# A hybrid SSD and attention layer: four gate tiles ahead of the merge, and the projection, its norms and the first feed-forward tiles in column halves

## What is computed

```python
hn = rmsnorm(x, p['norm_mix_pre']) * (1 + sc1) + sh1
proj = hn @ p['w_in']
z, xbc, dt, q, k, v, gates = jnp.split(proj, IN_SPLITS, axis=-1)
y_ssm, conv_new, h_new = ssm_branch(z, xbc, dt, conv_ctx, h0, p)
...
y_att = swa_prompt(q, k, v, sinks)
...
g_ssm, g_att = jnp.split(jax.nn.sigmoid(gates), 2, axis=-1)
merged = g_ssm * (y_ssm @ p['w_ssm_out']) + g_att * (y_att @ p['w_att_out'])
x = x + g1 * rmsnorm(merged @ p['w_out'], p['norm_mix_post'])
hn = rmsnorm(x, p['norm_ffn_pre']) * (1 + sc2) + sh2
gate, up = jnp.split(hn @ p['w_ffn_in'], 2, axis=-1)
gate, ffn_new = causal_dwconv(gate, ffn_ctx, p['ffn_conv_w'], p['ffn_conv_b'])
f = (jax.nn.silu(gate) * up) @ p['w_ffn_out']
x = x + g2 * rmsnorm(f, p['norm_ffn_post'])
```

## Time and profile before

| | |
|---|---|
| median of 3 runs (us) | 1429.63 (1429.2 to 1437.0) |
| profiled execution (us) | 1436.78 |
| its span, first to last instruction (us) | 1435.0 |
| mean granted clock of TensorE (share of full speed) | 0.959 |
| TensorE busy | 1339.5 us, 93% |
| VectorE busy | 809.9 us, 56% |
| ScalarE busy | 508.1 us, 35% |
| POOL busy | 530.9 us, 37% |
| DMA | 164.31 MB, mean 115 GB/s |

### The profile page before, as it was taken

One profiled execution on the slowest core, in us unless ns is written; L12 is line 12 of the kernel. 1 busy time (PEld: TensorE's weight loads), 2 busy tenths in 40 slices (PEclk: granted clock), 3 DMA queues, 4 the chain that ended last, 5 costly groups with the idle time before them and its releaser, 6 DMA issues. The chain is left out here.

```text
span 1435.0 us, 24802 instructions
## 1 busy us (share of the span) xinstructions
PE 1339.5 (93%) x10265; PEld 1255.5 (87%) x10265; DVE 809.9 (56%) x1288; ACT 508.1 (35%) x879; POOL 530.9 (37%) x315
## 2 busy tenths in 40 slices
PE   4699998999999999998798999988999999999996
PEld 1489988899899999998788999974899999999996
DVE  1745316898898898894780000337466666660105
ACT  2212425455455455453441222332332233332221
POOL 0533322332332333332464443332344444443443
PEclk8699989999999999999899999998799999999998
DMA  8275414433433433334331222541222222222221
GB/s 364 99 265 134 122 53 140 126 95 117 138 102 117 129 112 116 117 100 170 101 106 59 88 89 89 205 187 40 75 89 89 88 84 83 87 90 88 82 81 63
DMA packets 74015, 164.31 MB, mean 115 GB/s; under 512 B 28240, under 2 KB 42352, under 8 KB 70432
## 3 DMA queue, kind: packets, MB, share of 16 engines
q1 hardware_dynamic: 73904, 162.74, 35.2%
HBM read 147.10 MB, written 16.07 MB: 114 GB/s over the span
## 5 line engine op out<-in xcount | busy, mean ns | idle before, releaser
L161 POOL TENSOR_TENSOR w_lo<-raw_w,w_hi 128x1024 fp32r<-128x1024 f32 x174 | 429.0, 2466 | 730.3 <-ACT w_hi L155 730.3
L183 PE MATMUL psum<-hp_hi,w_hi 128*128 128x274 f32 x1472 | 449.8, 306 | 22.4 <-POOL hp_lo L284 13.4
L183 PE MATMUL psum<-hp_lo,w_hi 128*128 128x274 f32 x1472 | 430.9, 293 | 0.0
L183 PE MATMUL psum<-hp_hi,w_lo 128*128 128x274 f32 x1472 | 430.2, 292 | 0.0
L155 ACT ACTIVATE w_hi<-raw_w 128x1024 fp32r<-128x1024 f32 x174 | 184.1, 1058 | 547.0 <-PE psum L183 502.1
L183 PEld LDWEIGHTS psum<-hp_hi,w_hi 128*128 128x128 f32 x1472 | 281.7, 191 | 36.5 <-POOL hp_lo L284 16.1
L183 PEld LDWEIGHTS psum<-hp_lo,w_hi 128*128 128x128 f32 x1472 | 284.5, 193 | 1.3
L183 PEld LDWEIGHTS psum<-hp_hi,w_lo 128*128 128x128 f32 x1472 | 282.7, 192 | 0.0
L183 PE MATMUL psum<-hq_hi,w_hi 128*128 128x274 f32 x832 | 248.7, 299 | 12.5 <-POOL hq_lo L1677 8.5
L183 PE MATMUL psum<-hq_hi,w_lo 128*128 128x274 f32 x832 | 245.5, 295 | 0.0
L183 PE MATMUL psum<-hq_lo,w_hi 128*128 128x274 f32 x832 | 244.2, 294 | 0.0
(11 more groups left out here) (263 smaller groups left out, 2033.0 us busy)
## 6 DMA issues: line engine op xcount, KB each, us to landing
raw_w<-in_w_grp SPq DMA_DIRECT2D x58, 512.0 KB, 3.8
raw_w<-in_w_ffn_in SPq DMA_DIRECT2D x44, 512.0 KB, 3.6
ada<-in_w_ada SPq DMA_DIRECT2D x12, 1024.0 KB, 20.6
raw_w<-in_w_ffn_out SPq DMA_DIRECT2D x22, 512.0 KB, 3.5
acs_b<-mem_acs SPq DMA_DIRECT2D x8, 1096.0 KB, 5.6
raw_w<-in_w_ssm SPq DMA_DIRECT2D x16, 512.0 KB, 3.5
ada_o<-in_w_ada SPq DMA_DIRECT2D x4, 2048.0 KB, 11.3
raw_w<-in_w_qkv SPq DMA_DIRECT2D x13, 512.0 KB, 4.9
```

Of the source, the lines that this page charges most:

```text
L161: eng.tensor_tensor(flat(w_lo[self.hl_slot(n)]), raw_w[self.raw_slot(n)][:], flat(w_hi[self.hl_slot(n)]).bitcast(F32), ALU.subtract).then_ ...
L183: mm = pe.matmul(out[:, h, :], w, x[:, cols], start=first and j == 0, stop=last and j == 2)
```

## The change

It does five things.

- **Merge.** The Stream's order begins with the last attention gate tile and SSM gate tiles 0, 1 and 2 (`AHEAD = 3`); later SSM gates come three tiles ahead of their use, and each gate's Tanh has one of three buffers (`ths`). The SSM product of a tile comes ahead of the gate tile behind it. Loads of att and y are interleaved anew, POOL makes four of the eight low parts of att, the sums of squares sit at chosen blocks (`SUMS`), the reciprocal of y's norm goes to PSUM, and the first SSM tile waits for y's low parts block by block.
- **Border merge to projection.** The first column halves of projection tiles 0 and 1 are done in the merge's stage, their second halves behind the barrier.
- **Projection and norms.** Projection tiles 2 to 7 are done for columns 0 to 273 first, then for 274 to 547. Squares, sums, roots, reciprocals (into PSUM), residuals, modulations and splits work on halves (16 pieces instead of 8). Eight high/low pairs hold the weights of the half-done tiles (`plan`, `wait_free`: which pair, and what frees it). The modulation weights come as eight half loads through four smaller buffers.
- **Border to the feed-forward stage.** Feed-forward tiles 0 to 3 are done in the norms' stage: first halves behind the low parts of the first half, second halves block by block behind those of the second. From then on four high/low pairs are in rotation.
- **Output stage.** The turn of the rows of gate 2 and the few VectorE instructions on them move here; the extra pair `wx` for the last weight tile becomes one of the four.

The core of the diff:

```diff
+            def half(self, pe, out, n, k, hi, lo, h, done=None):
+                if k == 0:
+                    self.wait_split(pe, n)
+                wh, wl = w_hi[self.hl_slot(n)][:, k, :], w_lo[self.hl_slot(n)][:, k, :]
+                for j, (w, x) in enumerate(((wh, hi), (wh, lo), (wl, hi))):
+                    mm = pe.matmul(out, w, x[:, k, h * HW:(h + 1) * HW], start=k == 0 and j == 0, stop=k == KB - 1 and j == 2)
...
-            G1, A0 = 0, 1
+            G1, A0 = 0, 4
+            AHEAD = 3
-            src = [i["w_gate"][8 + KB - 1]] + [i["w_att"][m] for m in range(KB)]
+            src = [i["w_gate"][8 + KB - 1]] + [i["w_gate"][m] for m in range(AHEAD)] + [i["w_att"][m] for m in range(KB)]
             for m in range(KB):
-                src += [i["w_gate"][m], i["w_ssm"][2 * m], i["w_ssm"][2 * m + 1]]
+                src += [i["w_ssm"][2 * m], i["w_ssm"][2 * m + 1]]
+                if m + AHEAD < KB:
+                    src.append(i["w_gate"][m + AHEAD])
...
+            w.plan.update({O0 + n: (first, second, 4, 5, 6, 7, 2, 3)[n] for n in range(KB)})
+            w.plan.update({F0 + n: (first, second, 4, 5)[n] for n in range(4)})
+            for n in range(F0 + 4, END):
+                w.plan[n] = (2, 3, first, second)[(n - F0) % 4]
+                w.wait_free[n] = (w.used, n - 3)
...
-                        tile(2, hp_hi, hp_lo, sums=0)
+                        tile(0, hp_hi, hp_lo)
+                        tile(1, hp_hi, hp_lo, 0, 2)
+                        pe.wait_ge(ev_s, 1)
+                        tile(0, hp_hi, hp_lo, 1, 4)
+                        pe.wait_ge(th_s, 1)
+                        tile(1, hp_hi, hp_lo)
+                        SUMS = {(0, 0): 2, (0, 7): 3, (1, 7): 4, (3, 0): 5, (4, 1): 6, (5, 2): 7}
...
+                        for m in range(2, KB):
+                            pe.wait_ge(ev_s, evicted(0, m - 2))
+                            for k in range(KB):
+                                w.half(pe, psum[:, 2 * (m % 2), 0:HW], O0 + m, k, hp_hi, hp_lo, 0, w.used)
+                            if m >= 6:
+                                row_steps(m - 6)
+                        for m in range(2, KB):
+                            pe.wait_ge(ev_s, evicted(1, m - 2))
+                            for k in range(KB):
+                                w.half(pe, psum[:, 2 * (m % 2) + 1, 0:HW], O0 + m, k, hp_hi, hp_lo, 1, free_s)
+                                if (m, k) == (2, 3):
+                                    out_squares(0)
+                                elif (m, k) == (4, 3):
+                                    x_squares(2)
+                                elif (m, k) == (5, 3):
+                                    x_squares(7)
...
+                        for n in range(4):
+                            for k in range(KB):
+                                if n == 0:
+                                    pe.wait_ge(hlo_s, k + 1)
+                                w.half(pe, psum[:, ffn_bank(n), 0:HW], F0 + n, k, hq_hi, hq_lo, 0)
+                                if n == 0 and k == 4:
+                                    out_squares(1)
...
+                        for k in range(KB):
+                            pe.wait_ge(hlo_s, KB + k + 1)
+                            for n in range(3):
+                                w.half(pe, psum[:, ffn_bank(n) + 1, 0:HW], F0 + n, k, hq_hi, hq_lo, 1, w.used)
+                        for k in range(KB):
+                            w.half(pe, psum[:, ffn_bank(3) + 1, 0:HW], F0 + 3, k, hq_hi, hq_lo, 1, w.used)
```

707 lines of the change are left out of this document (472 added, 235 removed).

## The result

The kernel after takes **1392.35 us** (median of four, 1390.73 to 1394.64); the kernel before, in the same measurement, 1431.21 us (1429.2 to 1437.0). The ratio is 0.9723, 95% interval 0.969 to 0.9756: 39 us faster. The forecast was 1386 us. The profiled execution of after has a span of 1388.9 us against 1435.0.

The account below looks back on a forecast made before the run. TensorE's matmul units bound the kernel, so only its other time in merge and norms could be won: 24.1 + 25.6 - 4.2 - 1.8 = 43.7 us, 1436.8 to 1393 profiled, median 1386; range 1372 to 1404.

Parts of the forecast that it names:

- the two new costs: First feed-forward tiles behind the border lose 4.2 us; the last gate's turn, moved into the output stage, loses 1.8.
- the term of sum 3: Merge, end of attention tile 0: TensorE waits 2.7 us because add_squares(3) stands behind reciprocal(2).
- The other stalls: Merge: first Tanh about 0.5 us, sum 4 0.7, sums 5 to 7 0.3 each, first SSM tile 0.9.
- The wait of 4.9 for low parts of h: Norms, F0's first half block by block: 8.4 us for 3.06 + 0.42 of work, a wait of 4.9.
- The half costs: Norms, per column half: reciprocal 1.87 us, residual 0.88, modulation 0.75 free and 1.35 in the loop.
- Held residuals: Norms, first half: POOL's splits of F0+2 and F0+3 hold residuals by 0 to 4.8 us, taken as 4.
- Two waits: Behind the feed-forward border: 1.9 us for F0's eviction, then 2.3 for pair 0's gated product; 4.2 in all.
- The step from profile to median: Whole kernel: profile's 1436.8 us becomes 1393; the median, 7.2 lower before, goes from 1429.6 to 1386.
- (a): Rival, norms: the clock stays low through F0 to F3, about 20 us more, 1406 us; chance 0.13.
- (b): Rival, merge: VectorE's round still sets it, plus late low parts, 6 of the 24 us lost, 1395; chance 0.11.
- (c): Rival: everything is hidden, waits of 12.5 and the merge's 5.7 us mostly fall away, 1370 us; chance 0.08.
- (d): Rival, slower: the low clock stays in the feed-forward stage, 1517 us if throughout; chance 0.03.

Follow-up runs that it names:

- merge_only: The kernel before with the changed merge alone; projection, norms and feed-forward as they were: 1411.59 us, ratio 0.9852.
- ffn_first: The kernel after with tile F0 evicted ahead of the split of weight tile F0+6 behind the feed-forward border: 1394.63 us, ratio 0.9731.
- ffn2: The kernel after with fpar loaded and scaled at the norms' end and the splits of F0+6 and F0+7 behind the first Tanh: 1388.84 us, ratio 0.968.
- norms2: The kernel after with four shifts of order in border and norms (last low part's block, splits, eighth sum of x, last output square): 1390.5 us, ratio 0.9683.
- before_again: The kernel before, unchanged, in a second profiled execution: 1433.5 us, span 1431.7 us.
- sum3_split: The kernel after with sums 3 to 7 five to six blocks later and weight splits ahead of roots and y's low parts: 1394.37 us, ratio 0.973.
- lo_late: The kernel after with rounding and low parts of merged tiles 0 to 6 in one batch, as in the kernel before: 1395.88 us, ratio 0.9746.
- outsq_split: The kernel after with the split of F0+4 moved behind low part 7 of h and F0+5's behind the last: 1393.41 us, ratio 0.9717.
- resid: The kernel after with the splits of F0+2 and F0+3 behind the eighth square of x instead of among the residuals: 1391.96 us, ratio 0.9715.
- sum3_pool: The kernel after with POOL making the low parts of y's first group ahead of a weight split and an attention low part: 1387.79 us, ratio 0.9681.
- best: The kernel after with the edits of norms2, ffn2 and sum3_pool together: 1383.05 us, ratio 0.9636.

## Why the prediction was right, and where it was off

- **Where the time would come from** was right: the merge gave 21.2 on the profile's axis (forecast 24.1), projection to fourth tile 27.9 (25.6), the two new costs are 6.8 (6.0). The runs with each half alone confirm both as causes of their own.
- **The merge, 2.9 us short: the term of sum 3 was mis-sized.** Forecast 2.7 us; measured 3.87 of wait and 1.7 at the low clock behind it. The chain was named rightly (addition behind reciprocal 2), but the addition was counted at 1.7 us; beside four subtractions in a row on POOL it lasted 3.07. The 2.02 of the earlier trace rows was no upper bound, being one row beside other POOL work. The other stalls were 1.9 (forecast 3.0; sums 4 to 7 are not waited for), the first Tanh and the first SSM tile to within 0.1 us. That makes 1.8 of the 2.9; about 1 us has no place. In four other traces of the same merge (merge_only, ffn_first, ffn2, norms2) the addition lasted 1.73 to 1.74 and TensorE waited 2.53, close to the forecast; but in three of them the clock behind it was low for 6.8 us instead of 3.4, and the merge takes 217.2 again. The low clock behind this wait is the term that the forecast's merge put at nothing.
- **Projection and norms, 2.3 us better: right in size, wrong in place.** Taking its other terms off the 102.1 (units 73.4, row blocks 7.3, sums 7.6, turn 1.8) and the measured 2.2 at the border, 9.8 remain for waits and low clock, where it had 12.5. The wait of 4.9 for low parts of h does not exist; TensorE waits 3.6 at the output sum, one step earlier in VectorE's queue, and the low parts come in its shadow. The half costs were right: reciprocal 1.87, residual 0.9, modulation 0.8 free and 1.35 in the loop. Held residuals cost 3.7 (forecast 4), but moving them away brought nothing: the forecast had them on the path to the low parts of h, and TensorE's own order was the path.
- **The rule on two SBUF inputs** (the Trainium skill, SBUF — State Buffer, "Who interferes with whom"): by it the residuals are held and the products with a PSUM operand are not. The trace agrees: 2.55 and 2.14 against 0.50 us, and 0.43 us with a PSUM operand wherever POOL was busy. The same section counts COPY and TENSOR_SCALAR among those that can be held; the 2.26 us of a copy of two columns, 0.17 when free, agrees.
- **The table loads.** No drain is seen: the loads at 683.80 and 694.38 take 1.28 us, and the next ACTIVATE starts 1.29 us after each load's start, as in the earlier trace rows. The 2.66 us of the Trainium skill (ScalarE: Activation LUTs, "What ACT_TABLE_LOAD costs") is not what this trace shows.
- **Feed-forward border, 5.0 for 4.2.** Two waits were forecast (1.9 and 2.3) and came as 2.2 and 0.9, with 1.7 us of low clock between them. What counts is the end of the second, which VectorE's chain sets: forecast 10.5 us behind the border, measured 11.1, since its 2.3 us of copy beside a split had been left out. Reading the two waits as two costs leads to an edit like ffn_first, which shortens the first for nothing.
- **The step from profile to median** took 7.2 us off 1393, as if the new kernel had the same distance between the two. Of these, 2.8 stood in the merge of before, as far as one more execution tells (before_again), and this is the stage that the change replaces: they were counted as won and subtracted once more. This is the largest part of the 6.4 us by which the median misses the forecast. 1.6 more is the median of before itself (1431.2 here, 1429.6 then), 1.4 is the net gain by stage (42.3 for 43.7), and 0.6 has no place.
- **Rivals.** (a), the low clock through the four tiles, did not happen: they run from 944.4 to 984.2, at a mean clock of 0.96, with one low stretch of 3.4 us behind the wait for the output sum. (b) is half right: VectorE's round does set the merge's pace once the sums are moved (sum3_split), but in the kernel as written it costs one stall and not 6 us. (c) and (d) did not happen; the feed-forward stage runs at 1.00.

## What to carry to other kernels

When TensorE has found work for its waits, what is left is the order of single instructions on the engines beside it: look at the instruction that ends the wait, and at what its queue holds ahead of it that lasts longer than its free twin. Moving the consumer later only moves the wait if the producer's round is longer than the consumer's; ending the producer's first round earlier takes it away. And when two waits follow each other, add up to the second one's end before pricing the first, since shortening the first can be paid back whole.

## What the runs showed of the hardware

- **An instruction on VectorE that meets POOL's back-to-back work is let in at one of several ends.** The same addition beside the same four subtractions lasted 1.73 to 1.74 us (merge_only, ffn_first, ffn2, norms2) or 3.07 (after, lo_late, outsq_split, resid), one POOL instruction of 1.3 us apart; with only two subtractions left beside it, which had just ended, it lasted 0.71 (sum3_pool). Where it was let in early, one of POOL's own lasted about 1.85 instead of 1.37. The merge's code up to there is the same in all of these but sum3_pool.
- **The clock behind a wait of 1.80 us is not the same from one execution to the next.** In seven traces with the same wait for the last low part of the merge, the granted clock from there to the border was 1.00 in four (after, sum3_pool, resid, ffn_first; 3.7 us) and 0.67 in three (outsq_split, ffn2, sum3_split; 5.2 us), which costs 1.5 us. Behind 1.3 us (norms2) and 1.5 us (sum3_pool) it stayed, behind 3.67 it fell. A wait of 1.8 us in the output stage stands in all 14 traces, and the clock fell behind it in three (merge_only, ffn_first, best). What decides it, no trace shows. Such places and the start of the merge (664.8 to 671.4) differ by as much as the edits are worth, so edits worth 1 to 3 us had to be read from their stage; how much of the 3 to 7 us between the runs of one kernel they make is not shown. The two executions of the kernel before that have a trace differ by 3.3 us, 2.8 of it in the merge.
